# A hybrid attention and state-space layer on one core: output-norm scales applied behind w_out, attention's end set between w_out's first tiles, and another order of q norms and first transfers

## What is computed

```python
z = rmsnorm(x, p['attn_norm_g']) @ p['w_in']
q, k, v, u = split_projection(z)
q = rmsnorm(q, p['q_norm_g'])          # over each head's 64 channels
k = rmsnorm(k, p['k_norm_g'])
attn = windowed attention with ALiBi slopes and sinks, for prompt and samples
y_ssm, h_re, h_im = ssm_mixer(u, h0_re, h0_im, A_bar, B_bar, ...)   # a scan over tokens
g = jax.nn.gelu(y_ssm)
ssm_out = g * jax.nn.sigmoid(g @ w_glu + b_glu)
mix = jnp.concatenate([rmsnorm(attn, p['attn_out_g']),
                       rmsnorm(ssm_out, p['ssm_out_g'])], axis=-1)
h = x + mix @ p['w_out']
y = h + jnp.square(jax.nn.relu(rmsnorm(h, p['mlp_norm_g']) @ p['w_mlp_up'])) @ p['w_mlp_down']
```

## Time and profile before

| | us |
|---|---|
| median of 3 runs | 1202.09 |
| the three runs | 1201.89, 1202.09, 1203.55 |
| profiled execution, its own time | 1203.2 |
| span of the profiled execution | 1201.4 |
| TensorE busy in the span | 1188.0 |
| VectorE busy | 727.7 |
| ScalarE busy | 418.9 |
| GpSimd busy | 151.0 |

### The profile page before, as it was taken

One profiled execution on the slowest core, in us unless ns is written; L12 is line 12 of the kernel. 1 busy time (PEld: TensorE's weight loads), 2 busy tenths in 40 slices (PEclk: granted clock), 3 DMA queues, 4 the chain that ended last, 5 costly groups with the idle time before them and its releaser, 6 DMA issues.

```text
span 1201.4 us, 20141 instructions
## 1 busy us (share of the span) xinstructions
PE 1188.0 (99%) x8468; PEld 1111.5 (93%) x8468; DVE 727.7 (61%) x727; ACT 418.9 (35%) x507; POOL 151.0 (13%) x92
## 2 busy tenths in 40 slices
PE   9999999999999999999999999999999999999998
PEld 6676567679999999999999999999999999999998
DVE  8888889767655565555555555455555454555444
ACT  6110012565444433333333333333333333343331
POOL 2422513000000000001000011000011000010000
PEclk9999999998999999999999999999999999999999
DMA  7333223454645445454545454544445554545553
GB/s 284 135 123 111 79 91 106 152 135 139 210 160 172 142 160 191 163 171 158 169 165 175 159 173 152 179 163 166 168 158 170 170 170 160 174 141 171 180 171 119
DMA packets 54902, 190.27 MB, mean 158 GB/s; under 512 B 7832, under 2 KB 10008, under 8 KB 54424
## 3 DMA queue, kind: packets, MB, share of 16 engines
q1 hardware_dynamic: 54824, 189.09, 47.1%
HBM read 185.82 MB, written 5.28 MB: 159 GB/s over the span
## 4 chain that ended last, share of the span: by engine, by line
PE 95%; DVE 3%; ACT 0%; POOL 0%; issue 0%; DMA 0%; SPq 0%
PE psum L1278 94%; DVE states L698 1%; DVE turn L698 1%; DVE states L859 1%; POOL states L1203 0%; DMA w_raw<-in_w 0%; ACT gate L577 0%; PE psum L1401 0%; DVE sq L698 0%; DVE gate L1069 0%; DVE out_turn L901 0%; DVE out_turn L698 0%; DVE q_t L698 0%; ACT au L495 0%; ACT sq L583 0%
## 5 line engine op out<-in xcount | busy, mean ns | idle before, releaser
L689 DVE TENSOR_TENSOR w_lo<-w_raw,w_hi 128x1024 fp32r<-128x1024 f32 x288 | 402.6, 1409 | 402.8 <-ACT w_hi L432 402.1
L1278 PE MATMUL psum<-mov_b,w_hi 128*128 128x288 f32 x2560 | 508.2, 295 | 0.0
L432 ACT ACTIVATE w_hi<-w_raw 128x1024 fp32r<-128x1024 f32 x288 | 302.9, 1059 | 489.2 <-PE psum L1278 488.9
L1278 PEld LDWEIGHTS psum<-mov_b,w_hi 128*128 128x128 f32 x2560 | 409.6, 188 | 0.3 <-issue 0.2
L1278 PE MATMUL psum<-mov_a,w_hi 128*128 128x288 f32 x2048 | 406.6, 295 | 0.0
L1278 PE MATMUL psum<-mov_b,w_lo 128*128 128x288 f32 x1280 | 375.9, 294 | 0.0
L1278 PEld LDWEIGHTS psum<-mov_a,w_hi 128*128 128x128 f32 x2048 | 327.7, 188 | 0.1
L1278 PE MATMUL psum<-mov_a,w_lo 128*128 128x288 f32 x1024 | 300.7, 294 | 0.0
L1278 PEld LDWEIGHTS psum<-mov_b,w_lo 128*128 128x128 f32 x1280 | 241.6, 189 | 0.0
L1278 PEld LDWEIGHTS psum<-mov_a,w_lo 128*128 128x128 f32 x1024 | 193.3, 189 | 0.0
L1278 PE MATMUL psum<-x_g,w_raw 128*128 128x288 f32 x640 | 165.8, 417 | 3.4 <-DVE q_t L698 2.4
(11 more groups left out here) (175 smaller groups left out, 534.6 us busy)
## 6 DMA issues: line engine op xcount, KB each, us to landing
w_raw<-in_w SPq DMA_DIRECT2D x336, 512.0 KB, 3.3
h_t<-in_x SPq DMA_DIRECT2D x3, 576.0 KB, 8.2
out_y<-h_t SPq DMA_DIRECT2D x3, 576.0 KB
b_w<-in_b SPq DMA_DIRECT2D x1, 1024.0 KB, 5.5
c_w<-in_c SPq DMA_DIRECT2D x1, 1024.0 KB, 7.5
k_cache<-in_kc SPq DMA_DIRECT2D x1, 1024.0 KB, 5.5
v_cache<-in_vc SPq DMA_DIRECT2D x1, 1024.0 KB, 5.6
out_kc<-in_kc SPq DMA_DIRECT2D x1, 992.0 KB
```

The source lines that it names most:

```text
L432: nc.scalar.activation(hi3[:, n % SLOTS, :], raw3[:, n % SLOTS, :], ACT.Copy) \
L689: nc.vector.tensor_tensor(lo3[:, n % SLOTS, :], raw3[:, n % SLOTS, :], hi3[:, n % SLOTS, :].bitcast(F32), ALU.subtract) \
L1278: return nc.tensor.matmul(out, lhs_t, rhs, start=start, stop=stop)
```

## The change

1. w_out. The activations are no longer multiplied by the norms' factors. `mix_his` and `mix_los` split the raw values times the gains. Each group of w_out becomes two PSUM groups, one of the 8 SSM tiles (`wo0s` to `wo3s`) and one of the 8 attention tiles (`wo0a` to `wo3a`). `mix_out` multiplies each by its factor (`r_s` or `r_b`) and adds it to h, two VectorE instructions for each, eight times; before it was one addition for a group. The sums of squares are folded to one tile on VectorE, and TensorE needs one matmul on the ones for each instead of four.
2. Attention's end stands between w_out's first tiles: on TensorE the SSM tiles 0 to 7 of group 0 alternate with `pt2`, `spv`, the sum `rms_s`, `pt3` and `pv1`. Units are renumbered: `pt2`, `spv`, `rms_s`, `pt3`, `pv1` and `wo0a` now follow each other in the odd half. `hi_part` and `lo_part` of S_WO+2 to S_WO+6 come earlier.
3. q norms. `project_out("g_q0")` stands after two chunks of the scan instead of three; head means `qn1` come before `sc0`, and `gelu(1)` after `qn1`'s Exp.
4. First transfers. The first x tile is issued from ScalarE's queue, w step 0 in two transfers of one k-tile; the matmuls on zeros are ten of one pass instead of three of float32.

```diff
-            sp.dma_start(h_t[:, 0:TOK], ins["x"][:, 0:TOK]).then_inc(x_first, 16)
-            load_step(0)
+            sp.dma_start(raw4[:, 0, 0, :], ins["w"][0, :, 0:STEP_N]).then_inc(w_first, 16)
+            sp.dma_start(raw4[:, 0, 1, :], ins["w"][0, :, STEP_N:STEP_COLS]).then_inc(raw_loaded[0], 16)
...
+            act.dma_start(h_t[:, 0:TOK], ins["x"][:, 0:TOK]).then_inc(x_first, 16)
...
-            gelu(1)
             head_scale(UNIT["qn1"], au3, 4)
             unit_read(act, UNIT["qn1"])
             nc.scalar.activation(au3, au3, ACT.Exp, scale=-0.5).then_inc(rsqrt_ready, 1)
+            gelu(1)
...
-                    if k % 4 == 0:
-                        act.wait_ge(mix_scaled, (first + k) // 4 + 1)
+                    if k % 4 == 0 and first == 0:
+                        act.wait_ge(ssm_raw, k // 4 + 1)
+                    elif k % 4 == 0:
+                        unit_full(act, UNIT["pv1"])
+                        unit_read(act, UNIT[f"pv{k // 4}"])
+                        unit_read(act, UNIT["spv"])
...
             exps(2, 4)
+            mix_his(gate3, "g_ssm", 0, range(4))
             ssm_squares(0)
             exps(3, 5)
             sample_pt_out()
             hi_part(S_WO)
             hi_part(S_WO + 1)
             gate_out(1)
+            hi_part(S_WO + 2)
+            mix_his(gate3, "g_ssm", 0, range(4, QT))
             ssm_squares(1)
             pt_out(2)
-            root(r_s, UNIT["rms_s"], 0.25 / SSM_WIDTH, bank=3)
+            hi_part(S_WO + 3)
+            hi_part(S_WO + 4)
+            attention_squares(0)
+            root(r_s, UNIT["rms_s"], 0.25 / SSM_WIDTH)
+            hi_part(S_WO + 5)
             pt_out(3)
-            hi_part(S_WO + 2)
-            mix_his(gate3, "g_ssm", 0, range(4))
-            attention_squares(0)
-            mix_his(gate3, "g_ssm", 0, range(4, QT))
+            hi_part(S_WO + 6)
+            mix_his(q3, "g_attn", QT)
             attention_squares(1)
-            hi_part(S_WO + 3)
-            root(r_b, UNIT["rms_a"], 1.0 / ATTN_WIDTH)
-            hi_part(S_WO + 4)
-            mix_his(q3, "g_attn", QT, range(4))
-            hi_part(S_WO + 5)
-            mix_his(q3, "g_attn", QT, range(4, QT))
...
                 n = S_WO + GROUP_STEPS * g + SLOTS
-                hi_parts(range(n + 2 if g == 0 else n, n + GROUP_STEPS))
+                if g == 0:
+                    hi_parts(range(n + 3, n + 6))
+                    root(r_b, UNIT["rms_a"], 1.0 / ATTN_WIDTH)
+                    hi_parts(range(n + 6, n + GROUP_STEPS))
+                else:
+                    hi_parts(range(n, n + GROUP_STEPS))
...
-            scan(1, range(3))
+            scan(1, range(2))
             project_out("g_q0", q3[:, 0:4, :])
-            scan(1, range(3, 6))
+            scan(1, range(2, 6))
...
-            def add_squares(total, signal):
+            def add_squares(part, signal, total):
                 dve.wait_ge(signal, 2)
-                tt(total, total, au3, ALU.add).then_inc(squares_added, 1)
-            def mix_scale(part, buf):
-                tt(part, part, over_tiles(buf[:, :], 4), ALU.mult).then_inc(mix_scaled, 1)
+                link(tt(part, part, au3, ALU.add))
+                linked()
+                fold(part, total, True, squares_added)
...
+            def mix_out(name, g, r):
+                u = UNIT[f"wo{g}{name}"]
+                unit_full(dve, u)
+                tmp, part = sr4[:, "sa".index(name), :, :], h3[:, 4 * g:4 * g + 4, :]
+                tt(tmp, banks(u), over_tiles(r[:, :], OUTS), ALU.mult).then_inc(evacuated[u % 2], 1)
+                unit_read(dve, u)
+                summed = tt(part, part, tmp, ALU.add)
+                if name == "s":
+                    link(summed)
+                    linked()
+                else:
+                    summed.then_inc(h_added, 1)
             gate_mul(0)
             soft_max(3)
             soft_scale(2, 4)
+            mix_los(gate3, "g_ssm", 0, range(4))
             soft_scale(3, 5)
             lo_part(S_WO)
             lo_part(S_WO + 1)
             gate_mul(1)
             prompt_out(0)
-            add_squares(sq3, ssm_squared)
+            lo_part(S_WO + 2)
+            mix_los(gate3, "g_ssm", 0, range(4, QT))
+            add_squares(sq3, ssm_squared, ssq_s)
+            lo_part(S_WO + 3)
+            lo_part(S_WO + 4)
+            samples_out()
             one_over_root(UNIT["rms_s"], r_s)
-            mix_scale(gate3[:, 0:4, :], r_s)
-            mix_scale(gate3[:, 4:8, :], r_s)
-            samples_out()
-            mix_los(gate3, "g_ssm", 0, range(5))
+            lo_part(S_WO + 5)
+            lo_part(S_WO + 6)
             prompt_out(1)
-            mix_los(gate3, "g_ssm", 0, range(5, QT))
-            add_squares(sqa3, attn_squared)
-            lo_part(S_WO + 2)
-            lo_part(S_WO + 3)
-            one_over_root(UNIT["rms_a"], r_b)
-            mix_scale(q3[:, 0:4, :], r_b)
-            lo_part(S_WO + 4)
-            mix_los(q3, "g_attn", QT, range(2))
-            mix_scale(q3[:, 4:8, :], r_b)
-            mix_los(q3, "g_attn", QT, range(2, 4))
-            lo_part(S_WO + 5)
-            mix_los(q3, "g_attn", QT, range(4, QT))
...
-                lo_parts(range(n + 2 if g == 0 else n, n + GROUP_STEPS))
-                residual_out(g)
+                if g == 0:
+                    lo_part(n + 3)
+                    mix_out("s", g, r_s)
+                    lo_parts(range(n + 4, n + 6))
+                    one_over_root(UNIT["rms_a"], r_b)
+                    lo_parts(range(n + 6, n + GROUP_STEPS))
+                else:
+                    lo_parts(range(n, n + SLOTS))
+                    mix_out("s", g, r_s)
+                    lo_parts(range(n + SLOTS, n + GROUP_STEPS))
+                mix_out("a", g, r_b)
+                h_los(g)
...
-            nc.gpsimd.memset(au[:, 0:TOK], 0.0).then_inc(warm_filled, 1)
+            nc.gpsimd.memset(mov_b[:, 8192:8704].bitcast(F32), 0.0).then_inc(warm_filled, 1)
...
-            for _ in range(3):
-                mm(banks(UNIT["rms_x"])[:, 0, :], au[:, 0:P], au[:, 0:TOK])
+            zeros = mov_b[:, 8192:8704]
+            for cols in 4 * [512] + 6 * [TOK]:
+                mm(banks(UNIT["rms_x"], 1, 512)[:, 0, 0:cols], zeros[:, 0:P], zeros[:, 0:cols])
...
+            pe.wait_ge(squared, 3)
+            head_means("qn1", au3, 4).then_inc(psum_full, 1)
             pe.wait_ge(k_ready, 1)
             pe.wait_ge(q_ready, 1)
             scores(0)
-            pe.wait_ge(squared, 3)
-            head_means("qn1", au3, 4).then_inc(psum_full, 1)
             glu(0, range(0, 2))
             scores(1)
...
+            def mix(name, g, tiles):
+                first = QT * "sa".index(name)
+                gemm(UNIT[f"wo{g}{name}"], S_WO + GROUP_STEPS * g + first // STEP_K, HALF_STEPS, b4_of[name],
+                     ready=tiles_ready(mix_lo, before=first) if g == 0 else None, part=tiles)
+            mix("s", 0, range(1))
             turn_probs(2, 4)
-            sum_squares(UNIT["rms_s"], 3, sq3, 1)
-            turn_probs(3, 5)
+            mix("s", 0, range(1, 3))
             u = UNIT["spv"]
-            unit_read(pe, UNIT["pv0"])
+            unit_free(pe, u)
             unit_read(pe, UNIT["spt"])
             pe.wait_ge(vc_loaded, 16)
             for g in range(2):
@@ -1528,12 +1563,19 @@
                         done = mm(out[:, 16 * n:16 * n + 16], vc3[:, n, cols], pts[:, g, n, half, :],
                                   start=False, stop=n == DEC_BATCH - 1)
             done.then_inc(psum_full, 1)
+            mix("s", 0, range(3, 4))
+            sum_over_features(UNIT["rms_s"], ssq_s, squares_added, 1)
+            mix("s", 0, range(4, 5))
+            turn_probs(3, 5)
+            mix("s", 0, range(5, 6))
             attend(1)
-            gemm(UNIT["wo0"], S_WO, GROUP_STEPS, b4, ready=tiles_ready(mix_lo), part=range(4))
-            sum_squares(UNIT["rms_a"], 0, sqa3, 2)
-            gemm(UNIT["wo0"], S_WO, GROUP_STEPS, b4, ready=tiles_ready(mix_lo), part=range(4, KT))
+            mix("s", 0, range(6, QT))
+            mix("a", 0, range(5))
+            sum_over_features(UNIT["rms_a"], ssq, squares_added, 2)
+            mix("a", 0, range(5, QT))
             for g in range(1, 4):
-                gemm(UNIT[f"wo{g}"], S_WO + GROUP_STEPS * g, GROUP_STEPS, b4)
+                mix("s", g, range(QT))
+                mix("a", g, range(QT))
```

41 lines of the change are left out of this document (23 added, 18 removed), and 8 rows, old and new, of the table UNITS.

## The result

| | us |
|---|---|
| changed kernel, median of 12 runs | 1205.66 (1203.68 to 1207.69) |
| kernel before beside it, median of 12 runs | 1202.80 (1201.77 to 1203.70) |
| ratio, 95% interval | 1.0025 (1.0017 to 1.0032) |
| span of the profiled execution, before and after | 1201.4 and 1205.6 |
| forecast | 1201.0 (1197.5 to 1205.5) |

The change costs 2.9 us. The forecast was 4.7 us too low, and the time lies just above its range. 0.7 of the 4.7 us is the figure that it started from: three runs of the kernel before gave 1202.09, twelve give 1202.80. In a later comparison of the same two kernels the ratio was 1.0025 (1.0016 to 1.0034).

A forecast was written before the change was run, and what follows sets the result against it. From the samples' product with v on, TensorE works 928.0 us without pause, so only the end of w_out's first group counts. 2.6 gained less 1.4 lost is 1.2 us sooner; 1202.09 - 1.1 = 1201.0 us, range 1197.5 to 1205.5.

The forecast's parts named there:

- Start: First transfers and matmuls up to the sum on ssq: TensorE's earlier start is lost waiting there; 0, bounds -0.2 and +0.1.
- g_q0: Evacuation one scan chunk sooner: TensorE resumes 2.4 us sooner at full clock; 1.6 of 3.8 us remain after the square.
- q norms: Ahead of w_glu: the 1.3 us wait for Ln goes, 0.3 to 0.4 us of waiting comes at pt0's evacuation.
- w_out's start: From attend(0) to the first group's end: late S_WO+4 weights stall TensorE 7.0 us; 49.7 us instead of 48.35, 1.4 lost.
- qn0: Head means of q's first half: TensorE arrives at 179.5 us and gets the square at 181.7 us.
- Rival (b): The 2.2 us pause before qn0 halves the clock, losing the regained 1.5 us: 1202.4 us; chance 0.12.
- T: End of w_glu, where attend(0) starts: 260.9 us before, forecast 2.6 us sooner at 258.3.
- mix_out: Behind w_out's first group: extra VectorE instructions of 1.33 us, next low part still covered by 2.4 us; 0 taken.
- Rival (e): Clock stays at 1.2 GHz through pt3, tile 5 and attend(1), costing 4.2 us: 1205.2 us; chance 0.15.
- Rival (c): S_WO+4's weights land much sooner or the stall is absent: bound 1192.2 us, 1197 with half the stall; chance 0.15.
- T + 41: End of w_out's first group if TensorE had only its own work and nothing else waited; the kernel would win 9.9 us.

The follow-up runs named there:

- e10: Changed kernel with the x tile back on SyncE's queue, the rest of the new start kept; 1204.54 us, ratio 1.0018 to the kernel before.
- e1: Changed kernel with its start undone (x tile and w step 0 on SyncE, three float32 matmuls on zeros); 1204.50 us, ratio 1.0011.
- e12: Kernel before, unchanged, profiled once more; one run, span 1201.8 us.
- e15: Changed kernel with the old start and g_q0's evacuation after three chunks, so only q norms and w_out differ from before; 1204.38 us, ratio 1.0013.
- e2: Kernel before with the changed start alone; 1202.63 us, ratio 1.0000.
- e4: Kernel before with the five output transfers issued later, behind S_WO+15; 1202.16 us, ratio 0.9993.
- e8: Kernel before with only the evacuation of g_q0 one scan chunk sooner; 1202.24 us, ratio 1.0003.
- e3: Changed kernel with the five output transfers issued behind S_WO+15 instead of ahead of S_WO+4; 1199.19 us, ratio 0.9970 to the kernel before.
- e7: Changed kernel with hi_part and lo_part of S_WO+4 later, behind the root, pt_out(3) and the copy of spv; 1198.03 us, ratio 0.9965.
- e13: e3 with the four quarters of the samples' product set between w_out's tiles instead of in a row; 1199.11 us, ratio 0.9973.
- e16: e14 with ScalarE's root, hi_part(S_WO+5) and pt_out(3) ahead of attention's square; 1195.19 us, ratio 0.9936.
- e6: Changed kernel with head means qn0 behind eight k-tiles of g_q1 instead of six; 1203.96 us, ratio 1.0011.
- e14: e13 with the sum on ssq behind twelve k-tiles instead of ten and qn0 behind eight instead of six; 1196.39 us, ratio 0.9949.

## Why the prediction was wrong

The forecast's sum was 2.6 - 1.4 = 1.2 us sooner. By the profiles with falls taken out it is 0.0 - 2.4; by the runs 2.9 us later. So the steps ahead of w_out, counted at 2.6 us, gave nothing: the start took 0.7, g_q0 gave 1.9 less than was counted and the q norms 0.1 less. And w_out's start cost 1.0 us more than the 1.4 counted.

The 0.5 us between 2.4 and 2.9 lie inside the interval (2.0 to 3.8 us). Part of them may be more falls: read as a number of low stretches, the mean clock gives about 2.5 for a run of the kernel before (106 runs; both its profiles have 3) and 4.6 for one of the changed kernel (23 runs; both its profiles have 5). One or two of the 2.1 more belong to w_out's start (three stretches there in each of the changed kernel's profiles, two and one in those of before), where the 2.4 us count them already. Whether the rest stand ahead of w_out is open, since a run's mean doesn't say where.

- **Start: wrong.** "I take 0, with bounds of -0.2 (the constants land later beside x on the other queue)". The mechanism was named and sized too small: 0.7 (e10, e1). The step "whatever TensorE gains it waits for there" was right (2.15 us), but overlooked that such a wait can itself halve the clock: 1.7 us in both profiles of the changed kernel.
- **g_q0: wrong, the largest miss.** Of "2.4 us sooner" and "both are saved" the second part was no property of the code. The half clock in the earlier trace rows is there in some executions only: of the five profiles with this wait it follows in three (before, e12, e15), and e2 and e4 have 11.9 us behind the same 2.4 us. And the wait of 2.65 us that takes its place has the fall in four of nine. So without falls the step gains 2.4 and pays 2.65: forecast +1.6, measured -0.3 to -0.4 (e8).
- **qn0.** The wait was forecast at 2.2 us (181.7 against 179.5) and is 2.65. Rival (b), given 0.12, is what the changed kernel's profiles show.
- **q norms: right.** Wait gone, 0.41 us of wait come back at `sc2`, for `pt_head`; forecast 1.3 less 0.3, measured 0.9 (e15). The two added table loads cost ScalarE 1.28 us each and nothing else: the activation behind the one for `gelu(1)` starts 0.02 us after it, the one behind Exp's 0.01 us. Timeline of ScalarE in the changed kernel:

```profile
222.01 1.28 ACT L526 ACT_TABLE_LOAD   x1
223.31 1.16 ACT L526 ACTIVATE u_t<-u_t 128x1152 f32<-128x1152 f32 x1
```

(The Trainium skill, ScalarE: Activation LUTs, section What ACT_TABLE_LOAD costs, adds a drain of 1.38 us to a load; the trace of the changed kernel doesn't show it.)

- **w_out's start: mechanism right, size off by 1.0.** Landing T + 20.3 (forecast 20.4), sum T + 23.1 (23.25), tile 4 done T + 27.1 (27.4). Then `pt3` took 2.0 us to the next tile at half clock where 1.3 was taken, and the rest came to T + 50.8 instead of 49.7. The stop was 5.1 us, not 7, because tile 3 had already run at 0.50; that changed nothing, as the stop's end was fixed by the landing. That low stretch behind the samples' product, which the forecast knew from the earlier trace rows, was missing from its 16.2 us of work.
- **mix_out: right.** 908.77 us without a pause.
- **Rival (e): no.** `attend(1)` took 3.08 us; the clock came back while `pt3` ran (0.65 in the mean of 290 to 292 us). (The Trainium skill, TensorE: Matmul & The Clock Gate, Part 4: PE-mode transpose, says transposes don't count as busy for the gate; here they at least didn't keep the clock low.)
- **Rival (c): no** as to the landing, but much of what it priced was there to be had: with the weights out of the way 6.2 of the 50.8 us come back (e3, e7), with e13's and e16's order 7.5. The T + 41 of the work alone wasn't reached.
- **The starting figure.** The sum starts from 1202.09, the middle of three runs; with 1202.80 the same steps give 1201.7 us, still 4.0 too low.

## What to carry to other kernels

A stretch of low clock seen behind a pause in one profile may not be a price of that pause: profile the kernel twice, or take it out of both sums, before an edit is credited with it. When a step is split earlier, look at what queues behind it on the engine that splits, and at what is issued ahead of its transfer; moving either one freed 6 us here. And three runs are too few for a starting figure where runs lie 1.7 us apart. To remove a wait of 2 us on TensorE it was enough to put its small matmul two k-tiles later, where moving the producer earlier only moved the wait.

## What the runs showed of the hardware

- The granted clock fell to 0.50 for about 3.4 us behind 13 of 22 waits of 2.0 to 2.7 us between full-rate matmuls, behind none of the four waits of 0.4 to 1.7 us at `ssq`, and once behind a pause of 1.54 us (e16). It cost 1.7 us each time. The same code did it in one execution and not in another (the changed kernel against e3 and e7, the kernel before against e4).
- 5.6 us of products in a row, nearly all of 16 columns, went with a clock of 0.50 for 3.4 to 10 us in each of the 15 profiles that had them so (longer in e6 and e10, where the stop ahead of the sum followed); in the three profiles with the same products set one quarter at a time between tiles of 1.6 us it stayed at 1.00 there (e13, e14, e16).
- With the x tile's 144 KB issued on ScalarE's queue about when SyncE issued the constants' 90.5 KB (0.74 us), ScalarE first used the constants at 3.3 to 3.8 us (10 profiles), and at 2.7 to 2.8 us without (8 profiles).
- The load of S_WO+4, issued behind `out_vc` (a copy within DRAM) and the two `out_last`, landed 14.1 us after its issue in the changed kernel and 14.2 us in the kernel before, where the median of all 336 weight loads is 3.3 us. The issue of `out_vc` itself held SyncE for 3.56 us.
